# Five output-projection products moved into the last turn, and the order of loads around them

## The reference, cut to what matters

```
proj   = rmsnorm(x) @ w_in                  # LRU branch, RWKV-7 branch, two gates
merged = sigmoid(gate_lru) * out_lru + sigmoid(gate_rwkv) * out_rwkv
x      = x + merged @ w_out                 # the output projection
x      = x + hier_moe(rmsnorm(x))           # 32 experts of width 256, two per row
y      = rmsnorm(x) * final_norm            # and seven state outputs
```

## Time and profile before

| what | us |
|---|---|
| three runs | 777.09, 779.16, 780.55 |
| median of the three | 779.16 |
| the profiled execution's own time | 778.58 |
| its span in the trace | 776.70 |
| turn 7 up to the first output-projection product | 442.2 to 489.6 |
| output projection, first to last product of tile 1 | 489.6 to 518.2 |
| experts, first up-projection to last down-projection | 548.9 to 762.5 |

### The profile page before, as it was taken

How to read it: one execution, slowest core, us unless ns; L and a number is a source line. 1 busy time by engine, 2 the same in 40 slices (tenths; PEclk the granted TensorE clock), 3 DMA queues, 4 the chain that set the end, 5 groups by cost and what they waited for, 6 DMA issues and landing times.

```text
span 776.7 us, 18145 instructions
## 1 busy us (share of the span) xinstructions
PE 745.7 (96%) x7047; PEld 461.2 (59%) x7047; DVE 443.2 (57%) x1173; ACT 240.9 (31%) x593; POOL 61.3 (8%) x71
## 2 busy tenths in 40 slices
PE   5999999999999999999999999999899999999896
PEld 4566666666666676666666666445455555555442
DVE  4455677777777767867767774515523433223225
ACT  4233353452552452443433443231101001000014
POOL 3000000400000000000000000000122222131110
PEclk9999999999999999999999999999999999999999
DMA  9542161870160251151251541898799999999995
GB/s 252 142 120 70 29 173 35 159 196 14 40 187 7 65 165 27 41 164 27 63 142 27 207 186 35 279 400 332 317 413 415 422 418 418 420 420 419 420 393 183
DMA packets 117126, 160.06 MB, mean 206 GB/s; under 512 B 27686, under 2 KB 92000, under 8 KB 110664
## 3 DMA queue, kind: packets, MB, share of 16 engines
q1 hardware_dynamic: 100532, 147.57, 52.8%
q0 software_dynamic: 5760, 7.80, 3.8%
q10 hardware_dynamic: 10789, 4.06, 2.0%
HBM read 154.43 MB, written 15.73 MB: 219 GB/s over the span
## 4 chain that ended last, share of the span: by engine, by line
PE 88%; DMA 4%; DVE 3%; ACT 2%; issue 1%; SPq 1%; ACTq 1%; POOLq 0%; DVEq 0%
PE bank L807 24%; PE bank L1220 13%; PE bank L1227 6%; PE bank L979 5%; PE bank L813 5%; PE bank L1113 4%; PE bank L1057 4%; DMA scratch<-in_exp_up 3%; PE bank L779 2%; PE bank L1259 2%; PE bank L921 2%; PE bank L912 2%; PE bank L1009 1%; PE bank L841 1%; PE bank L1084 1%
## 5 line engine op out<-in xcount | busy, mean ns | idle before, releaser
L807 PE MATMUL bank<-xnT,wall 128*128 128x320 f32 x656 | 194.7, 441 | 0.0
L807 PEld LDWEIGHTS bank<-xnT,wall 128*128 128x128 f32 x656 | 118.6, 190 | 45.1 <-issue 2.6
L695 POOL DMA_INDIRECT merged<-xn2d,gidx x15 | 15.6, 1037 | 518.9 <-DVE gidx L2160 410.4
L2204 DVE COPY vecs<-bank 128x512 f32<-128x512 f32 x32 | 22.1, 691 | 56.7 <-PE bank L1227 30.4
L2209 DVE TENSOR_TENSOR scratch<-bank,n 128x512 f32<-128x512 f32 x30 | 20.5, 687 | 48.8 <-PE bank L1220 45.2
L979 PE MATMUL bank<-xnT,wall 128*128 128x320 f32 x128 | 47.9, 456 | 0.3
L1652 ACT ACTIVATE vecs<-bank 128x128 f32<-128x128 f32 x32 | 8.9, 278 | 117.2 <-PE bank L1220 117.2
L1220 PE MATMUL bank<-scratch 128*64 128x256 f32 x320 | 38.4, 395 | 3.7 <-DMA scratch<-in_exp_up 3.3
L1220 PE MATMUL bank<-vecs,scratch 128*64 128x256 f32 x352 | 40.6, 382 | 0.5 <-DVE scratch L2145 0.5
L1419 ACT ACTIVATE shared<-bank 128x256 f32<-128x256 f32 x32 | 12.3, 386 | 73.4 <-PE bank L807 66.7
L1057 PE MATMUL bank<-xnT,wall 128*128 128x320 f32 x112 | 33.1, 439 | 0.7
(11 more groups left out here) (433 smaller groups left out, 1357.4 us busy)
## 6 DMA issues: line engine op xcount, KB each, us to landing
wall<-in_w_in SPq DMA_DIRECT2D x58, 512.0 KB, 5.4
scratch<-in_exp_gate SPq DMA_DIRECT2D x10, 1024.0 KB, 14.3
scratch<-in_exp_up SPq DMA_DIRECT2D x10, 1024.0 KB, 16.5
vecs<-in_exp_gate SPq DMA_DIRECT2D x10, 1024.0 KB, 10.2
vecs<-in_exp_up SPq DMA_DIRECT2D x10, 1024.0 KB, 12.5
scratch<-in_exp_down SPq DMA_DIRECT2D x6, 1024.0 KB, 13.8
shared<-in_exp_gate SPq DMA_DIRECT2D x10, 512.0 KB, 14.9
shared<-in_exp_up SPq DMA_DIRECT2D x10, 512.0 KB, 17.2
```

The costliest lines, as they stand in the source:

```text
L695: pool.indirect_dma_start(rows, None, xn2d, bass.IndirectOffsetOnAxis(ap=e, axis=0), bounds_check=N - 1, oob_is_err=False).then_inc(S(sem) ...
L807: q = mm(tpbank(L, name), wbuf[name][:, k, :], xnT[:, k, :], start=(k == 0), stop=(k == KC - 1))
L2204: CP(ye[:, e % 2, :], bank[6 + e % 2][:]).then_inc(S("ye"), 1)
```

## The change: what it does

Five of the 16 products of tile 0 (chunk 2 both halves, chunk 3 both halves, chunk 4 first half) are computed inside turn 7, each in the place of one `unread` product, into banks 6 and 7. VectorE adds the two sums to x there (into `osum`, which lies in free parts of `shared` and in `rtb`), after `level_w(4)`. TensorE waits for that addition before it reuses the banks. After the turn, `out(0)` does the other 11 products, with chunk 7 moved behind the transposes and behind chunks 0 and 1 of tile 1. The loads are reordered so that chunks 2 to 4 of `w_out` and x's first tile come first, expert 0's gate and up weights come before chunks 5 and 6, and expert 5's wait until `osum` has been read.

```diff
+PARTS = [(2, 0), (2, 1), (3, 0), (3, 1), (4, 0)]
+        osum = [shared[0][:, 0:512], rtb[:]]
# SyncE
+            def load_out(names):
+
+                for n in names:
+                    j = list(COL).index(n)
+                    sp.wait_ge(S("tp"), FULL.made(PAIRS - 2, n) if n in NEXT else LAST.made(PAIRS - 1, n))
+                    sp.dma_start(wo[j], a["w_out"][0, j * P:j * P + P, :]).then_inc(S("w_" + n), 16)
+
+            load_out(("r", "k", "v"))
+            sp.wait_ge(S("mixed"), 3 * PAIRS + 3)
+            for h in range(2):
+                sp.dma_start(osum[h], a["x_prompt"][0, 0:P, 512 * h:512 * h + 512]).then_inc(S("x1_in"), 16)
             gu6 = [gu_src(name, RING) for name in ("exp_gate", "exp_up")]
             for g in range(2):
                 sp.dma_start(once_gu[:, g].rearrange("p k f -> p (k f)"), gu6[g][:, 0:(KC - 1) * DE]).then_inc(S("ew6"), 16)
             load_gu(3, 3)
-            for j, n in enumerate(COL):
-                sp.wait_ge(S("tp"), FULL.made(PAIRS - 2, n) if n in NEXT else LAST.made(PAIRS - 1, n))
-                sp.dma_start(wo[j], a["w_out"][0, j * P:j * P + P, :]).then_inc(S("w_" + n), 16)
+            load_out(("lx", "ly"))
             sp.wait_ge(S("tm_ps"), 3 * PAIRS)
             sp.wait_ge(S("lvW"), 5 * (PAIRS - 1) + 4)
             load_gu(0, 0)
+            load_out(("gl", "gr"))
...
-            sp.dma_start(x1[:, 0:2, :], a["x_prompt"][0].rearrange("(t p) d -> p t d", p=P)).then_inc(S("x1_in"), 16)
+            sp.dma_start(x1[:, 1, :], a["x_prompt"][0, P:2 * P, :]).then_inc(S("x1_in"), 16)
...
             sp.wait_ge(S("wkv_out"), 80 * PAIRS)
+            sp.wait_ge(S("x1r"), 1)
             load_gu(5, 5)
# TensorE, turn 7
                         if n != "r" or half:
-                            unread(bank[6][:, 0:256], 1)
+                            out_part(2 * "rkv".index(n) + half - 1)
                         needs()
+                def out_part(j):
+
+                    k, h = PARTS[j]
+                    if h == 0:
+                        pe.wait_ge(S("w_" + list(COL)[k]), 16 * (PAIRS + 1))
+                    mine = [x for x, y in PARTS if y == h]
+                    q = mm(bank[6 + h][:], merged[:, k, 0:P], wo[k][:, 512 * h:512 * h + 512], start=(k == mine[0]), stop=(k == mine[-1]))
+                    if j == len(PARTS) - 1:
+                        q.then_inc(S("wo_ps"), 1)
...
                 def u_needs():
                     pe.wait_ge(S("akv_c"), i + 1)
+                    if last:
+                        pe.wait_ge(S("rw_n"), 1)
# TensorE, output projection
                     for h in range(2):
+                        if t == 0 and (k, h) in PARTS:
+                            continue
...
-            out(0, 0, KC)
+            out(0, 0, KC - 1)
+            pe.wait_ge(S("merged"), PAIRS)
 
             for c in range(KC):
                 q = tr(bank[1 if c < 4 else 5][0:36, 128 * (c % 4):128 * (c % 4) + 128], lastL[:, c, :], ident)
             q.then_inc(S("rowL_ps"), 1)
-            out(1, 0, KC)
+            out(1, 0, 2)
+            out(0, KC - 1, KC)
+            out(1, 2, KC)
# VectorE, turn 7
                 level_w(4)
+                if last:
+                    dve.wait_ge(S("x1_in"), 32)
+                    dve.wait_ge(S("wo_ps"), 1)
+                    for h in range(2):
+                        q = TT(osum[h], osum[h], bank[6 + h][:], ADD)
+                    q.then_inc(S("rw_n"), 1)
# VectorE, after the turns
-                    q = TT(x, x, ob[2 * t + h][:], ADD)
+                    q = TT(x, osum[h] if t == 0 else x, ob[2 * t + h][:], ADD)
```

More of the change, by code:

```diff
@@ L592, in _ @@
             sp.wait_ge(S("wkv_out"), 80 * PAIRS)
+            sp.wait_ge(S("x1r"), 1)
             load_gu(5, 5)
-            sp.wait_ge(S("wo_ps"), 3)
+            sp.wait_ge(S("wo_ps"), 4)
             load_gu(4, 4)
-            sp.wait_ge(S("wo_ps"), 4)
+            sp.wait_ge(S("wo_ps"), 5)
             load_dn(1, 1)
@@ L1163, in _ @@
             pe.wait_ge(S("rowP_c"), 1)
-            pe.wait_ge(S("rw_n"), 1)
+            pe.wait_ge(S("rw_n"), 2)
             logits(0)
@@ L2040, in _ @@
             ob = [bank[j] for j in (0, 3, 4, 6, 2)]
-            dve.wait_ge(S("x1_in"), 16 * 3)
             def inverse(t):
@@ L2064, in _ @@
             for t in range(3):
-                dve.wait_ge(S("wo_ps"), t + 1 if t < 2 else 4)
+                dve.wait_ge(S("wo_ps"), t + 2 if t < 2 else 5)
+                if t == 0:
+                    dve.wait_ge(S("rw_n"), 1)
+                if t == 1:
+                    dve.wait_ge(S("x1_in"), 16 * 5)
                 for h in range(2 if t < 2 else 1):
```

## The result

The changed kernel takes 773.37 us (median of 11 runs, 770.36 to 777.41), the kernel before in as many runs beside it 778.54 us (774.17 to 780.55). The ratio is 0.9944, with an interval from 0.9929 to 0.9959. The forecast was 773.6 with a range of 771.7 to 777.0, so the time is right. The profiled execution of after is its slowest, 777.41 us with a span of 775.5, which is why the two spans lie only 1.2 us apart (776.7 before).

What follows compares the result with a forecast made beforehand. The prediction took TensorE, busy 96% of the span, as the bound. It summed 4.38 - 0.88 + 2.10 = 5.60 us off a profiled 778.58, giving 772.98, and forecast a median of 773.6, range 771.7 to 777.0.

Steps and rivals of the forecast that it cites:

- Part 1: Output projection, tile 0: five products leave `out(0)`, 4.38 us less on the path, with chunk 7's weights there in time.
- Part 2: Last turn: five products replace `unread` ones; the first three hidden, the fourth and fifth cost 0.88 us.
- The mark that the prediction set, 15.6: Last turn: `level_x(2)` still starts 15.6 us after the turn's start, as a sign that the forecast holds.
- Part 3: Last turn's levels: filling TensorE's idle time keeps the clock at full, gain 2.10 us.
- Rival 1: Last turn's levels: clock falls anyway, or too rarely for before's median to hold the 2.10; 775.5 us, chance 0.24.
- Part 4: VectorE's two additions, 1.4 us, hidden in its 2.50 us wait ahead of `level_x(4)`, with 1.1 left.
- Part 5: Reordered loads of `w_out`, x and expert weights: nothing on the path, 0, between -0.5 and +1 us.
- Part 6: Expert stream: it shifts with TensorE, so gains reach the end; the 2.80 us late wait and slow 5.36 us stay.
- Rivals 2 and 3: Rival 2: transfers hold the end, 779.2, 0.10; rival 3: clock stays low through last turn's levels, 780.9, 0.10 with like losses.

Runs made afterwards that it cites:

- e5_again: The changed kernel run once more, unchanged, beside 35 executions of the kernel before: median 773.99 us, ratio to before 0.9965.
- e3_chunk7: The changed kernel with chunk 7 of tile 0 back ahead of the transposes and tile 1: median 777.38 us, ratio to before 1.0028.
- e4_loads: The kernel before with the new order of the `w_out` and expert 0 loads alone, no product moved: median 778.86 us, ratio to before 1.0008.
- e2_nofill: The kernel before without the five `unread` products in the last turn's levels: median 779.90 us, ratio to before 1.0030.
- e6_late: The changed kernel with four more `unread` products ahead of the second normalisation: median 777.69 us, ratio to before 1.0011.
- e8_six: The changed kernel with a sixth product (chunk 4, second half) in the turn and VectorE's second addition moved back: median 773.93 us, ratio to before 0.9960.
- e7_fill3: The changed kernel with three instead of five `unread` products behind the router's logits: median 775.48 us, ratio to before 0.9974.
- e1_double: The kernel before with each of the last turn's five `unread` products doubled: median 778.38 us, ratio to before 1.0016.

## Why the prediction was right or wrong

**Part 1 (4.38) held.** 28.60 became 24.32, 4.28, in after and in e5_again alike. 27 products took 7.99 + 15.45 = 23.44 us, 0.868 each, against (14.00 + 13.73) / 32 = 0.867 before. (The counts x32 and x36 are two matmul instructions for each product, not a product and its weight load as I read them; the number of products is the same. One `unread` product is x2 in TensorE's own timeline.) No DMA wait stood at chunk 7: it was issued at 497.07, 1.2 later than in the earlier trace rows because the turn was later, and was needed near 503 (two chunks of tile 1, 3.4 us, behind 499.62). The prediction held that chunk 7 would be there in time with 2.3 us to spare and did not price the kernel without its move; e3_chunk7 puts the price of leaving it out at 2.13 in the chain.

**Part 2 (+0.88) was short: +1.06 in after, 1.4 on average.** The fourth and fifth products cost what was said: from the end of `level_x(2)`'s group to the projection it is 3.53 us in after (460.50 to 464.03) and 2.67 in e4_loads (460.91 to 463.58), +0.86. The cover of the first three was over-read. The prediction let `level_w(2)` be late by one product's 0.44; two new products stand ahead of it, and the idle 0.18 covers little of them. Its start went from 13.29 us after the turn's start in e4_loads to 13.90. With the third product's 0.43, TensorE is 1.04 later against 0.83 of idle time: 0.2 too late, and `level_x(2)` starts 15.82 after the turn's start instead of 15.62. The mark that the prediction set, 15.6, was missed by this 0.2. The pause inside `level_x(2)`, which after does not have and e4_loads does not have, puts up to 0.54 more on it: the levels of the six profiles with the change average 20.2, 1.4 above e4_loads (1.6 in e5_again).

**Part 3 (2.10) is the step that failed, as a gain of the kernel.** In the two profiles it looks right: 1.00 where it was 0.57, the idle piece gone, the levels 0.79 shorter (1.85 less 1.06; forecast 1.2). But e4_loads has the old filling and the old gap and no fall, and over the executions the mean clock of the change equals that of before (0.9957 and 0.9948 against 0.9949 and 0.9948, errors 0.0009 to 0.0004). The prediction took a fall that one profile showed for a property of the program. What stays open is what the new products do to the clock. None of the six profiles that have them shows the fall in the levels, one of the two with the old filling does. And against e4_loads, which has the same order of the `w_out` and expert 0 loads and none of the moved products, the mean clock of the change's 23 executions is higher, 0.9952 against 0.9927 (errors 0.0006 and 0.0004), and the mean time 4.1 us lower (± 0.5), about 1 us more than the stages give. So the products may well save some of the clock that the new order of loads may cost; no run has the products without the new order, and against before nothing is left. Rival 1 had named this, "in so few executions that the median of before does not hold the 2.10", and is the mechanism that the runs bear out, with 0.24 against my 0.56. The size was off too: 5.04 - 3.20 = 1.84, not 2.10, because I put starts of the timeline (0.44 for the transposes, 0.46 for the first group) beside pieces of the chain (0.53 for both). The reason given for the step, that filling holds the clock, is not false: e2_nofill shows it, at 2.4 us. What failed is that the stretch's fall was entered as a gain of every execution: against before, the mean clock gained 0.0008 in one batch and nothing in the other, each within its error.

The Trainium skill, "TensorE: Matmul & The Clock Gate", section "Why this matters for your kernels", lays a fall of the clock to idle gaps longer than any between two products here; the longest is the 2.80 us of the earlier trace rows. e4_loads agrees with it that a gap of 0.82 us need not bring a fall. e2_nofill does not: the clock fell there behind one gap of 1.05 us, ahead of a group of small products at 457.87 (in the timeline the transposes behind that group already take 1.03 us, against 0.61 for those before it). By that section alone neither the filling nor its removal should have mattered; by the runs its removal costs some 2.5 us.

**Part 4 held.** Two additions of 0.68 us at 466.97 and 467.56; VectorE still waits 1.31 us for TensorE ahead of `level_x(4)` (said 1.1, from 2.50).

**Part 5 held on the path**: e4_loads, nothing at equal clock. By the means it is 1.15 us slower (± 0.42), about the +1 that was allowed, and by the slope all of it goes with the lower clock. The DMA share from 540 to 547 fell from 0.39 to 0.03, so the pause did get longer.

**Part 6 held**: e6_late, and the 183 to 184 us of the stream in every profile. The late wait was to stay at 2.80 us and is 2.06, which is most of the -0.81 in the table. Whether the up-projection behind it comes at the low clock (5.36 us) changes from execution to execution: in e4_loads and e6_late the same group takes 3.67, and a further 0.7 us goes to a wait at the next expert.

**How the time came out right all the same.** By stages the change is worth 4.28 - 1.06 = 3.2 us in after, and 4.28 - 1.4 = 2.9 with the average of the six profiles. At equal clock it is 2.7 to 2.9. Over all executions the mean of after is 774.05 (23 executions) and that of before 777.21 (81), 3.2 again. The first 11 executions of after had a mean clock of 0.9957, and the difference was 4.4 in the means and 5.2 in the medians there, 2.7 and 3.1 in e5_again. So 773.6 was met with some 1 to 2 us of luck. Rival 1's 775.5, less the 1.4 by which before itself is lower in the later groups (777.1 for 778.5), is 774.1, and e5_again gave 773.99. Why the first batch had the higher clock, chance or the chip it ran on, stays open.

**Rivals 2 and 3** fell: the stream moves with TensorE, and no profile of the changed kernel or of a variant of it has a low clock over the levels.

## What to carry to other kernels

A stretch at half clock in one profile is one execution. Before its removal is entered as a gain, look at the mean time and the mean granted clock of many executions with and without the supposed cause, and hold the recorded clock against the pace of equal products: it left a slow start out in four of ten profiles here. A part of the change that costs nothing on the path (here the order of the loads) can still go with a lower clock, so it needs its own count too. Products moved from a stretch where TensorE is alone into the place of idle time or of filling are worth their full time less what filling took, as long as the last wait of the emptied stretch (here the weights of chunk 7) is moved back as well: without that, half of the gain goes into it. To place products in cover, add up all that stand ahead of each wait on the chain and set them against the idle time there, not one at a time; and take durations for one sum from one view.

## What was not expected of the hardware

- The lower clock comes in the same program at different places from one execution to the next: in the levels (before, not e4_loads), behind the logits (after, e4_loads, e6_late, e8_six; not before, e5_again), in the late up-projection (5.36 us or 3.67). Two stretches could be priced: 1.85 us with a pause of 0.17 in it (levels) and 2.83 us (logits). The correlation of mean granted clock and time within one kernel lies between -0.26 (e2_nofill) and -0.95 (after's first 11 executions), -0.75 over all.
- The length of the gap ahead did not decide it. Behind the late wait of 2.06 us the clock fell in after, e3_chunk7 and e7_fill3 and not in e5_again and e8_six, nor behind 2.46 to 2.61 us in e1_double, e4_loads and e6_late.
- The record of the granted clock can miss a slow stretch at the start: 8 to 10 matmul instructions of one group from 14 to 18 us at a recorded 1.00 in four profiles, 9 at a recorded 0.57 in two, 16 or 17 at 1.00 in four.
- In after's 530 to 534 the clock was 0.50 with TensorE busy for all of the 4 us. The idle time ahead of it was one wait of 0.47 us for ScalarE.
- The expert stream's length, 183.06 to 183.87 us from its first load to the late up-projection, did not change while its start lay anywhere from 542.67 (e5_again) to 549.97 (e2_nofill).
